# Output of a chunked state-space scan: from tokens on the partitions to features on the partitions

## The reference

```
xc = x * dt                                     # per token and head
cs = cumsum(dt * a)                             # within a chunk of 128 tokens
cb = einsum('bclgn,bcsgn->bclsg', cc, bc)
lmat = exp(where(lower, cs_l - cs_s, -inf))
y = (einsum('bclsg,bclsgr,bcsgrp->bclgrp', cb, lmat, xc)          # within the chunk
     + einsum('bclgn,bcgrpn,bclgr->bclgrp', cc, h_in, exp(cs)))   # from the chunk before
y = yf + reversed(yb) + ssd_d[:, None] * xs     # both directions, and the skip
ssd = rmsnorm(y * silu(z), ssd_norm_g) @ w_ssd_o
merged = sigmoid(ga) * (att @ w_attn_o) + sigmoid(gs) * ssd
```

## Time and profile before

| | us |
|---|---|
| median of 3 runs (3241.51 to 3247.06) | 3247.01 |
| the profiled execution | 3242.14 |
| its span, first to last instruction | 3240.3 |
| PE busy | 3098.7 (96%) |
| DVE busy | 1217.1 (38%) |
| ACT busy | 708.5 (22%) |
| POOL busy | 543.6 (17%) |

### The profile page before, as it was taken

One profiled execution on the slowest core, in us unless ns is written; L12 is line 12 of the kernel. 1 busy time (PEld: TensorE's weight loads), 2 busy tenths in 40 slices (PEclk: granted clock), 3 DMA queues, 4 the chain that ended last, 5 costly groups with the idle time before them and its releaser, 6 DMA issues.

```text
span 3240.3 us, 36148 instructions
## 1 busy us (share of the span) xinstructions
PE 3098.7 (96%) x14146; PEld 2397.0 (74%) x14146; DVE 1217.1 (38%) x2380; ACT 708.5 (22%) x1599; POOL 543.6 (17%) x562
## 2 busy tenths in 40 slices
PE   8998899999989999999999999999988999989998
PEld 7766788887854546767758688887876666678887
DVE  1344232213245545556533443343236555541100
ACT  1112221101022323444430120111013234440100
POOL 0000100003200002121213334342210122210100
PEclk9999899999999799999999999999999999999999
DMA  6454234442235122222212222222211323324342
GB/s 242 156 222 181 104 143 155 149 142 85 78 143 196 51 106 91 91 104 91 78 66 78 78 78 91 79 91 79 104 65 40 118 98 104 104 98 144 142 150 97
DMA packets 60831, 365.69 MB, mean 113 GB/s; under 512 B 5818, under 2 KB 17146, under 8 KB 18320
## 3 DMA queue, kind: packets, MB, share of 16 engines
q1 hardware_dynamic: 48768, 334.65, 28.7%
q10 hardware_dynamic: 10944, 25.36, 2.1%
q0 software_dynamic: 976, 3.67, 0.3%
HBM read 362.38 MB, written 1.28 MB: 112 GB/s over the span
## 4 chain that ended last, share of the span: by engine, by line
PE 87%; DVE 9%; ACT 2%; issue 1%; DMA 0%; POOL 0%; POOLq 0%; DVEq 0%; ACTq 0%
PE PB L1146 11%; PE PB L349 11%; PE PB L466 9%; PE PB L393 9%; PE PB L975 7%; PE PA L466 6%; PE PB L868 5%; PE PS L466 4%; PE PB L1127 4%; PE PB L1044 3%; DVE work L2175 2%; PE PA L1220 2%; PE PB L1158 2%; PE PA L1196 1%; PE PA L1209 1%
## 5 line engine op out<-in xcount | busy, mean ns | idle before, releaser
L1146 PE MATMUL PB<-H,ring 128*128 128x512 f32 (+1 forms) x1024 | 430.7, 568 | 0.0
L1146 PEld LDWEIGHTS PB<-H,ring 128*128 128x128 f32 x1024 | 193.2, 191 | 182.2 <-issue 176.0
L393 PE MATMUL PB<-work,ring 128*128 128x256 f32 x1280 | 277.7, 379 | 1.2 <-ACT work L1700 1.2
L393 PEld LDWEIGHTS PB<-work,ring 128*128 128x128 f32 x1280 | 243.1, 190 | 34.5 <-issue 1.5
L349 PE MATMUL PB<-H,ring 128*128 128x256 f32 x960 | 209.9, 381 | 10.4 <-ACT H L1493 7.5
L975 PE MATMUL PB<-H,ring 128*128 128x256 f32 x992 | 214.3, 379 | 0.0
L349 PEld LDWEIGHTS PB<-H,ring 128*128 128x128 f32 x960 | 183.2, 191 | 37.1 <-issue 12.0
L975 PEld LDWEIGHTS PB<-H,ring 128*128 128x128 f32 x992 | 188.5, 190 | 25.6
L2175 DVE SCALAR_TENSOR_TENSOR work<-PB,par,work 128x510 f32<-128x510 f32 (+3 forms) x256 | 182.2, 713 | 14.8 <-ACT work L1588 8.0
L868 PE MATMUL PB<-H,ring 128*128 128x256 f32 (+1 forms) x640 | 178.8, 434 | 0.9 <-ACT mod L1381 0.9
L1127 PE MATMUL PB<-ring,H 128*128 128x256 f32 x768 | 174.5, 382 | 4.9 <-DVE work L2175 4.9
(11 more groups left out here) (329 smaller groups left out, 4491.3 us busy)
## 6 DMA issues: line engine op xcount, KB each, us to landing
ring<-stream SPq DMA_DIRECT2D x315, 1024.0 KB, 4.8
sums<-cs_rows ACTq DMA_DIRECT2D x16, 1024.0 KB, 4.6
sums<-cs_rows ACTq DMA_DIRECT2D x16, 512.0 KB, 3.9
work<-scratch POOLq DMA_DIRECT2D x1, 2560.0 KB, 14.1
X<-xT SPq DMA_DIRECT2D x2, 1024.0 KB, 13.3
out<-H SPq DMA_DIRECT2D x1, 1024.0 KB, 4.8
con<-consts SPq DMA_DIRECT2D x1, 716.0 KB, 18.1
wdt<-w_dt POOLq DMA_DIRECT2D x1, 512.0 KB, 10.5
```

What stands on the lines that cost most here:

```text
L393: mm = pe.matmul(PB[:, pair, t, 0:T], ring[:, c % SLOTS, k, t * P:(t + 1) * P], rhs(KT * part + k), start=(part == 0 and k == 0), stop=(pa ...
L1146: mm = pe.matmul(PB[:, pair, t, 0:Tc], ring[:, c % SLOTS, k, t * P:(t + 1) * P], H[:, k, 0:Tc], start=(k == 0), stop=(k == KT - 1))
```

## The change

The output of the scan now has features on the partitions and tokens along the free axis, from the product on. Two heads form a unit (with two chunks of tokens; 4 units in a group of layer 0, 2 in one of layer 1). `XC` (64 columns) is stationary and the masked scores move (128 columns); the first head's product goes to partitions 0 to 63 of `PA`, the second's to 64 to 127. The incoming state's product has `HT` stationary; its weights exp(cs) must then stand in rows, and ACT makes them from the fetched rows (`row_exps`, `EC`). The skip moves from POOL to DVE as one instruction for each pair of heads. The gate projection is turned round likewise. The norm is split: ACT applies the gain group by group and squares the product (`gain`), POOL adds the squares up (`squares`), PE sums over partitions with one product of ones, and the root is multiplied into the second gate `GS`. The 16 tiles need no turning.

```diff
+        def scan_units(la):
+            return [(q, t0) for q in range(2) for t0 in ((0, 2) if la == 0 else (0,))]
@@ PE @@
-                        col = CHUNK * (t % per)
-                        for k in range(KT):
-                            mm = pe.matmul(PB[:, pair, t // per, col:col + CHUNK], H[:, k, t * P:(t + 1) * P],
-                                           ring[:, c % SLOTS, k, :], start=(k == 0), stop=(k == KT - 1))
-                        if t == T // P - 1:
+                        for k in range(KT // per * s_, KT // per * (s_ + 1)):
+                            mm = pe.matmul(PB[:, pair, t, 0:T], ring[:, c % SLOTS, k, t * P:(t + 1) * P], H[:, k, 0:T],
+                                           start=(k == 0), stop=(k == KT - 1))
+                        if n == 2 * per - 1:
                             mm.then_inc(chunk_done, 1)
...
-                                pe.matmul(PA[1][:, 256 * d:256 * d + 256], CV[b][:, 3, t * P:(t + 1) * P], HT[d],
-                                          start=True, stop=True).then_inc(sem("s_inter"), 1)
+                                for q in range(2):
+                                    mm = pe.matmul(PA[1][:, 256 * d + P * q:256 * d + P * q + P],
+                                                   HT[d][:, P * q:P * q + P], CV[b][:, 3, t * P:(t + 1) * P],
+                                                   start=True, stop=True)
+                                mm.then_inc(sem("s_inter"), 1)
...
                             pe.wait_ge(sem("s_inter_read"), LAYER["s_inter_read"] * la + inter_count(la, g, 2))
-                        for t in tok:
+                        for t in range(2):
+                            cols = slice((t0 + t) * P, (t0 + t + 1) * P)
                             for d in range(2):
-                                mm = pe.matmul(PA[t // 2][:, 256 * (t % 2) + HD * r:256 * (t % 2) + HD * r + HD],
-                                               MB[r % 2][:, d, t, :], XC[r % 2][:, d, t, :],
-                                               start=(d == 0), stop=(d == 1))
+                                for r in range(2):
+                                    mm = pe.matmul(PA[q][HD * r:HD * r + HD, cols], XC[n % 2][:, d, t, r, :],
+                                                   MB[n % 2][:, r, d, t, :], start=(d == 0), stop=(d == 1),
+                                                   skip_group_check=True)
                         mm.then_inc(sem("s_within"), 1)
...
-                for i in range(16):
...
-                        mm = pe.transpose(yt_bank(i)[:, t * P:(t + 1) * P], Y[:, t, i * P:(i + 1) * P], ident)
-                    mm.then_inc(sem("yt"), 1)
...
+                for n in range(4):
+                    project_gs(1, n // 2, n % 2)
+                pe.wait_ge(sem("s_y"), LAYER["s_y"] * (la + 1))
+                pe.wait_ge(sem("s_sum"), LAYER["s_sum"] * (la + 1))
+                pe.matmul(PA[0][:, 0:T], full(ONE), SQ_SUM[:, 0:T], start=True, stop=True).then_inc(sem("z_sum"), 1)
+                for n in range(8):
+                    project_gs(2 + n // 4, n // 2 % 2, n % 2)
+                pe.wait_ge(sem("z_root"), LAYER["z_root"] * (la + 1))
@@ ACT @@
+                def row_exps(g):
+                    for i in range(3):
+                        for d, order in enumerate((F_ORDER, B_ORDER)):
+                            t = order[i + 1]
+                            if not live(la, t):
+                                continue
+                            for r in range(2):
+                                half = slice(HD * r, HD * r + HD)
+                                ins = copy(EC[half, i, d, :].rearrange("p (a b) -> p a b", a=2),
+                                           BC[half, :, r, d, t * P:(t + 1) * P], ACT.Exp)
+                    ins.then_inc(sem("s_rows"), 1)
...
+                def decay_exps(g, u):
...
+                            hh = 32 * d + 4 * g + 2 * q + r
+                            for t in range(2):
+                                ins = copy(MB[n % 2][:, r, d, t, :], BC[:, q, r, d, (t0 + t) * P:(t0 + t + 1) * P], ACT.Relu,
+                                           scale=-1.0, bias=CS[:, t0 + t, hh:hh + 1])
+                    ins.then_inc(sem("s_fall"), 1)
+                    act.wait_ge(sem("s_fall"), LAYER["s_fall"] * la + n + 1)
+                    copy(MB[n % 2], MB[n % 2], ACT.Exp, scale=-1.0).then_inc(sem("s_exp"), 1)
...
+                def gain(g):
+                    act.wait_ge(sem("s_z"), LAYER["s_z"] * la + g + 1)
+                    for i in range(2):
+                        copy(Y[:, 2 * g + i, 0:T], ZT[:, i, 0:T], ACT.Copy, scale=p_(f"ssd_g{la}", 2 * g + i))\
+                            .then_inc(sem("s_scaled"), 1)
+                    act.wait_ge(sem("s_scaled"), 16 * la + 2 * (g + 1))
+                    copy(ZT[:, :, 0:T], ZT[:, :, 0:T], ACT.Square).then_inc(sem("s_gain"), 1)
...
+                    row_exps(g)
+                    half = len(units) // 2
+                    for u in range(half):
+                        decay_exps(g, u)
+                    if g >= 1:
+                        gain(g - 1)
...
+                gain(SSD_GROUPS - 1)
+                act.wait_ge(sem("s_y"), LAYER["s_y"] * (la + 1))
+                act.wait_ge(sem("z_sum"), la + 1)
+                copy(RSTD[:, 0:T], PA[0][:, 0:T], ACT.Sqrt, scale=1.0 / SSD_INNER, bias=EPS_C).then_inc(sem("z_root"), 1)
@@ DVE @@
-                            then(vec.tensor_tensor(YT2[d].rearrange("p (a b) -> p a b", a=4),
-                                                   PA[1][:, 256 * d:256 * d + 256].rearrange("p (a b) -> p a b", a=4),
-                                                   ECS[:, t, heads].unsqueeze(2).broadcast_to([P, 4, HD]), ALU.mult))
-                            vec.tensor_tensor(YI[:, t, :], YI[:, t, :], YT2[d], ALU.add)\
-                                .then_inc(sem("s_inter_read"), 1)
+                            e = EC[:, i, d, :].rearrange("p (a b) -> p a b", a=2)
+                            to = Y[:, 2 * g:2 * g + 2, t * P:(t + 1) * P]
+                            got = PA[1][:, 256 * d:256 * d + 256].rearrange("p (a b) -> p a b", a=2)
+                            if i < 2:
+                                vec.tensor_tensor(to, got, e, ALU.mult).then_inc(sem("s_inter_read"), 1)
+                            else:
+                                then(vec.tensor_tensor(e, got, e, ALU.mult))
+                                vec.tensor_tensor(to, to, e, ALU.add).then_inc(sem("s_inter_read"), 1)
+                    v.wait_ge(sem("s_inter_read"), LAYER["s_inter_read"] * la + inter_count(la, g, 2))
+                    for i in range(2):
+                        ins = vec.scalar_tensor_tensor(Y[:, 2 * g + i, 0:T], CV[g % 2][:, i, 0:T], p_(f"ssd_d{la}", 2 * g + i),
+                                                       Y[:, 2 * g + i, 0:T], ALU.mult, ALU.add)
+                    then(ins)
...
+                def masked(g, u):
...
+                    v.wait_ge(sem("s_exp"), LAYER["s_exp"] * la + n + 1)
+                    if u == 0:
+                        v.wait_ge(sem("s_cbm"), LAYER["s_cbm"] * la + 2 * g + 2)
+                    m = MB[n % 2].rearrange("p r d t n -> p r d (t n)")
+                    cb = CBM[:, :, t0:t0 + 2, :].rearrange("p d t n -> p d (t n)")
+                    vec.tensor_tensor(m, m, cb.unsqueeze(1).broadcast_to([P, 2, 2, 2 * P]), ALU.mult)\
+                        .then_inc(sem("s_m"), 1)
...
-                    y = Y[:, tok, CHUNK * g:CHUNK * (g + 1)]
-                    vec.tensor_tensor(y, y, ZT[:, 0:T // P * CHUNK].rearrange("p (a b) -> p a b", a=T // P), ALU.mult)\
-                        .then_inc(sem("z_used"), 1)
+                    vec.tensor_tensor(ZT[:, :, 0:T], Y[:, 2 * g:2 * g + 2, 0:T], ZT[:, :, 0:T], ALU.mult)\
+                        .then_inc(sem("s_z"), 1)
...
+                        dve_turn(v, Y[:, 8 * part:8 * part + 8, :], [YT[:, n, 4 * part:4 * part + 4, :] for n in range(4)], 4,
+                                 lambda: None, sem("y_turned"))
+                v.wait_ge(sem("z_root"), la + 1)
+                then(vec.reciprocal(RSTD[:, 0:T], RSTD[:, 0:T]))
+                for j, (pair, before) in enumerate(GROUPS[f"gs{la}"]):
                     v.wait_ge(evacuated[pair], 2 * before + 2)
+                    for t in range(2):
+                        gate = GS[:, 2 * j + t, 0:T]
+                        vec.tensor_tensor(gate, gate, RSTD[:, 0:T], ALU.mult).then_inc(sem("gs_scaled"), 1)
@@ POOL @@
+                def squares(g):
+                    pool.wait_ge(sem("s_gain"), LAYER["s_gain"] * la + g + 1)
+                    a, b = ZT[:, 0, 0:T], ZT[:, 1, 0:T]
+                    sum_ = SQ_SUM[:, 0:T]
+                    gp.tensor_tensor(sum_, a if g == 0 else sum_, b, ALU.add)\
+                        .then_inc(sem("s_sum" if g == 0 else "s_sum_half"), 1)
+                    if g:
```

(31 more changed lines are left out.)

211 lines of the change are left out of this document (75 added, 136 removed).

## The result

The changed kernel took 3226.95 us (median of 4 runs, 3225.78 to 3230.29), the kernel before 3246.92 beside it: ratio 0.9944, estimated from all runs of both (the two medians alone give 0.9938), 95% interval 0.9927 to 0.9961. The forecast was 3221 with a range of 3205 to 3238. The profiled execution took 3225.78 us with a span of 3224.0, which is 16.3 less than the span before.

The account below looks back on a forecast made before the run. PE bounds the kernel, 87% of the span. Layer 0 9.6, layer 1 2.1 and 2.4, tails 5.3 and 3.7 sum to 23.1 us off 3242.1, so 3219; forecast put at 3221, range 3205 to 3238.

Parts of the forecast that it names:

- The unit: Products within a chunk: 16 rows on PE take 1.2 us instead of 1.73, 0.53 saved a unit.
- gate projection: Layer 0's gate projection, now with 512 moving columns: four pieces in 8 groups save 2.2 us.
- The rival with halves that don't overlap: Units on PE: column halves run serially, a unit takes 2.03 us, time 3255; chance 0.08.
- The rival without switch cost: Units on PE: no switch, 14 us more saved, time 3207; chance 0.14, shared with the hidden skip.
- units' 17.0: Layer 0: 32 units at 0.53 us saved each give 17.0 us.
- The wait for the masked scores: Layer 0: PE waits about 1.2 us at the first unit in each of 8 groups, 9.6 us lost.
- ACT's exponentials: Layer 0: 12 new exponentials on ACT, about 0.33 us each, counted at nothing.
- 7 x 0.3 = 2.1 us: Layer 1's regular groups: each takes 41.65 us instead of 41.95, saving 2.1 us in seven.
- eight waits lower the clock: Part of the worse-wait rival, layer 0: one doubling (1.5 us on 8 groups) costs 12 us, time 3233; chance 0.16.
- The last group: Layer 1's last group, without taps: PE's stretch takes 11.3 us instead of 12.66; with the seven groups' 2.1, listed as 2.4.
- The tails: Ends of both layers: layer 0's falls from 56.2 to 50.9 us (5.3 saved), layer 1's from 30.5 to 26.8 (3.7).
- The drain with each table load: Both tails: by the skill page's 1.38 us per load, they give 5.5 us less and the whole 3227.

Follow-up runs that it names:

- repeated unit: Changed kernel, but in layer 1 TensorE does each regular group's first two-headed unit three times over; 3223.94 us.
- early taps: Changed kernel, but in layer 1 the taps of the next group's first tile go ahead of the third reading of the states; 3205.14 us.
- pairs: Changed kernel, but a unit's eight matmuls alternate between the column halves in pairs, not one by one; 3231.00 us.
- sigmoids first: Changed kernel, but ScalarE takes the first gate pair's two sigmoids ahead of its wait for the norm's sum and root; 3222.44 us.
- skip twice: Changed kernel, but the skip term's two multiply-adds run twice in layer 0; 3255.25 us.
- heads in turn: Changed kernel, but a unit's two heads go one after the other, four matmuls each, instead of side by side; 3244.72 us.
- skip early: Changed kernel, but the skip term's two multiply-adds go ahead of the third reading of the states; 3209.29 us.
- all three together: Changed kernel with skip term early in layer 0, next group's first-tile taps early in layer 1, first gate pair's sigmoids ahead of the root; 3189.26 us.

## Why the prediction was right

**The unit.** I put it at 1.2 us: 0.86 for eight overlapped rounds and 0.3 for the switch, from matmuls in four column parts and two row halves. It is 1.03 us to the next start and 0.16 on the product behind: (0.37 + 0.28 of the gate projection's forecast saving) / 4 a unit, so 1.19. The rival with halves that don't overlap is out: sixteen rows at 0.108 one after another are 1.73, and the unit takes 1.03; with the four matmuls of each head in a row it grew to 1.48. The rival without switch cost is out by the 0.16 and by 1.03 against 0.86.

**The gate projection.** Its 2.2 us stand in the ledger together with the units' 17.0, and the sum was met to 0.3. That part and the switch can't be told apart in these rows.

**The wait for the masked scores.** Forecast 1.24, measured 1.26 us, eight times. The working from DVE's rows held to the second digit, and moving or doubling the two instructions moved the wait by as much. ACT's exponentials, counted at nothing, cost nothing: with the skip term moved, 0.2 us of waits are left.

**Layer 1, and the step that was mis-sized.** "7 x 0.3 = 2.1 us" came out as 1.6 - 5.0 = -3.4. The mechanism was right: the gate projection waits about 2 us for the taps in every group (14.9 in seven), and an undisturbed group takes 41.72 us, forecast 41.65. What I left out was the clock. I did have the rival "eight waits lower the clock", and argued against it that the waits of 0.71 us had left the clock up. That was a reading from waits a third as long as those I was forecasting myself, and it was aimed at layer 0, where waits of 1.26 us indeed did nothing. The trace before gave no warning either: its last group of layer 1 has one wait of 2.15 us, and the clock stayed at 1.00 behind it. It happened in layer 1, and the repeated unit and the early taps show that the idle time did it. Why in three groups of seven, when the wait is 2.13 or 2.14 us in all of them, stays open. This term makes 5.5 of the 7 us between the forecast sum and the measured one.

**The last group** met its 2.4 us.

**The tails.** 5.3 and 3.7 us forecast, 4.9 and 3.4 measured. The wait was forecast at 4.7 and measured 4.61, and 3.9 against 3.96; the remaining 0.4 us in layer 0 are small errors in three terms: the clock took 2.9 us instead of 2.7 (30.50 for two chunks where 27.63 stand at full clock), and the first chunk, the product of ones and the two chunks at full clock 0.1 each. That the waits hang on the order of root and sigmoids was shown by turning it round.

**The drain with each table load**, which the Trainium skill (ScalarE: Activation LUTs, What ACT_TABLE_LOAD costs) counts at 1.38 us, is not in the trace: the load of 1647.85 is 1.28 long and the root starts at 1649.14. That the figure of 3227 which that page would give is near the median is chance; the tails did not lose 5.5 us, layer 1's clock lost 5.0.

**What the median adds.** The profiled executions differ by 16.4 us, the medians by 20.0. Both lie in the interval, 12.7 to 23.7 us. Against the median before, the forecast sum of 23 is inside it, against the profiled one it is 7 too large.

## What to carry to other kernels

When an edit lengthens the work ahead of something that TensorE waits for, price not only the wait but the clock behind it. In the regular groups of these scans, waits up to 1.7 us cost only themselves, waits of 2.1 us cost 1.7 us more in three cases of seven, and those of 2.5 us 1.6 us more in seven of eight. That is no safe limit elsewhere: between the scans of the kernel after, the clock also fell behind one wait of 1.76 us (at 2412.35), and not behind two others of that length. Then look where the same engine idles a few instructions earlier: two instructions moved into an idle stretch gave back nearly as much (17.7 us) as the whole change had brought (20.0). And judge an edit at its own place first, because unchanged work elsewhere can take back several microseconds through the clock.

## What the runs showed of the hardware

- Products of 64 columns at opposite halves of the array overlap even when the order of issue is not one by one: eight matmuls took 1.03 us alternating singly, 1.07 in pairs, and 1.48 in fours. In the last case, as read from the starts of the rows, the second half's rows began when five of the first half's eight had begun.
- Equal waits did not always have the same effect. Four traces have the waits of 2.1 us in layer 1 (after, pairs, sigmoids first, skip twice), and in each the clock fell in three of the seven groups; with waits of 1.65 us or less (before, heads in turn, skip early, repeated unit), or none (early taps, all three together), it fell in none.
- The stretches at half clock behind a wait were 3.41 us long in the scans' groups, and 6.8 behind the 4.6 us wait of layer 0's tail; filling the idle time with repeated products kept the clock up (292.0 for 297.1 us, with more work).
- The work between the scans, with the same instructions and waits, took 860.0 us in the traces of the kernels before, after, with early taps and with the repeated unit, but 863.3 to 863.6 with the heads in turn, the pairs, the early skip and all three together, 864.8 with the sigmoids first, and 866.0 with the skip twice. Of that stretch 13.7 us are at half clock in the first four, 20.5 in the next four, 23.9 and 30.7 in the last two. Why the same waits lower the clock for longer in one kernel than in the other stays open. It isn't only when that work starts within the execution: in the kernel after and in that with the pairs it starts at 1684.20 in both, and takes 860.0 and 863.6 us.
